# The modulation vector of an adaLN block, computed with its output features on the partitions and moved into two stages of the kernel

## The reference

```python
def adaln_params(cond, w, b):
    mod = jax.nn.silu(cond) @ w + b            # (1024) @ (1024, 6144)
    return jnp.split(mod[..., None, :], 6, axis=-1)

sh1, sc1, g1, sh2, sc2, g2 = adaln_params(c, mod_w[i], mod_b[i])
h_lat = modulate(rmsnorm(x, norm_g[i, 0]), sh1, sc1)      # h * (1 + scale) + shift
x = x + g1 * hyena_mix(h_lat, p)
x = x + g2 * conv_ffn(modulate(rmsnorm(x, norm_g[i, 1]), sh2, sc2), *ffn_p, rows, GRID_W)
```

## Time and profile before

| | |
|---|---|
| median of 3 runs | 1061.96 us (1061.87 to 1062.69) |
| the profiled execution | 1061.37 us |
| its span | 1059.3 us |
| busy share: PE, DVE, ACT, POOL | 98%, 63%, 40%, 51% |
| data moved | 131.9 MB, mean 125 GB/s |

### The profile page before, as it was taken

The page is one execution under the profiler, slowest core; times in us unless marked ns, Lnnn a source line. Parts: engine busy times, 40 slices in busy tenths (PEclk is TensorE's granted clock), DMA queues, the critical chain, the costliest instruction groups (busy, mean ns, idle before and its releaser), DMA issues.

```text
span 1059.3 us, 13471 instructions
## 1 busy us (share of the span) xinstructions
PE 1040.0 (98%) x4968; PEld 856.4 (81%) x4968; DVE 665.7 (63%) x1007; ACT 418.6 (40%) x687; POOL 543.7 (51%) x401
## 2 busy tenths in 40 slices
PE   7999999999999999999999999999999999999996
PEld 5889887877877888778888888778888888888885
DVE  5663776866499765985788847386666666520503
ACT  6223547665554243644444342442323223221222
POOL 1688895999200064234444346535465545553641
PEclk9999999999999999999999999999999999999999
DMA  6446454342446922212322113303222232223222
GB/s 257 164 168 225 133 187 153 90 163 70 179 159 238 379 104 100 93 67 80 110 83 84 54 42 155 143 33 146 87 80 79 103 135 79 80 80 135 104 80 79
DMA packets 19611, 131.92 MB, mean 125 GB/s; under 512 B 3411, under 2 KB 3811, under 8 KB 13030
## 3 DMA queue, kind: packets, MB, share of 16 engines
q1 hardware_dynamic: 8784, 92.62, 23.2%
q0 software_dynamic: 6560, 27.27, 8.0%
q10 hardware_dynamic: 4214, 11.30, 2.8%
HBM read 124.90 MB, written 6.30 MB: 124 GB/s over the span
## 4 chain that ended last, share of the span: by engine, by line
PE 95%; DVE 2%; ACT 1%; DMA 1%; issue 0%; POOL 0%; SPq 0%; POOLq 0%; ACTq 0%; DVEq 0%
PE bank L505 81%; PE bank L496 7%; PE bank L511 3%; PE bank L752 1%; PE bank L746 1%; DMA x_sb<-x_in 1%; PE bank L904 1%; PE bank L741 1%; DVE arena L2178 0%; DVE arena L2181 0%; PE bank L913 0%; PE bank L753 0%; PE bank L869 0%; ACT arena L1189 0%; DVE arena L2214 0%
## 5 line engine op out<-in xcount | busy, mean ns | idle before, releaser
L1730 POOL TENSOR_TENSOR ring_parts<-ring,ring_parts 128x1024 fp32r<-128x1024 f32 x102 | 248.7, 2442 | 266.3 <-ACT ring_parts L1189 263.5
L505 PE MATMUL bank<-hT_parts,ring_parts 128*128 128x512 f32 x1344 | 339.2, 393 | 0.8 <-ACT hT_parts L1518 0.8
L1189 ACT ACTIVATE ring_parts<-ring 128x1024 fp32r<-128x1024 f32 (+2 forms) x163 | 168.6, 1043 | 383.7 <-PE bank L505 219.9
L505 PEld LDWEIGHTS bank<-hT_parts,ring_parts 128*128 128x128 f32 x1344 | 249.6, 188 | 54.7 <-ACT hT_parts L1518 2.4
L505 PE MATMUL bank<-ring_parts,hT_parts 128*128 128x512 f32 (+1 forms) x672 | 171.6, 379 | 1.0 <-POOL ring_parts L1730 0.6
L505 PE MATMUL bank<-ring_parts,arena_parts 128*128 128x512 f32 (+1 forms) x736 | 172.4, 386 | 0.0
L505 PEld LDWEIGHTS bank<-ring_parts,arena_parts 128*128 128x128 f32 x736 | 136.6, 188 | 27.9 <-DVE arena L2416 0.3
L505 PE MATMUL bank<-arena_parts,ring_parts 128*128 128x512 f32 x592 | 148.0, 391 | 0.3 <-DVE arena_parts L2285 0.3
L505 PEld LDWEIGHTS bank<-ring_parts,hT_parts 128*128 128x128 f32 x672 | 122.4, 188 | 22.8 <-POOL ring_parts L1730 1.0
L2521 DVE SCALAR_TENSOR_TENSOR arena<-bank,small,arena 128x441 f32<-128x441 f32 (+2 forms) x176 | 122.3, 695 | 24.6 <-DVE arena L2521 1.7
L505 PEld LDWEIGHTS bank<-arena_parts,ring_parts 128*128 128x128 f32 x592 | 111.0, 188 | 25.4 <-DVE arena_parts L2285 2.1
(11 more groups left out here) (223 smaller groups left out, 1100.5 us busy)
## 6 DMA issues: line engine op xcount, KB each, us to landing
ring<-weights_in SPq DMA_DIRECT2D x39, 2048.0 KB, 8.0
arena<-mod_w_in POOLq DMA_DIRECT2D x32, 512.0 KB, 4.1
arena<-mod_w_in POOLq DMA_DIRECT2D x8, 1024.0 KB, 5.5
x_sb<-x_in SPq DMA_DIRECT2D x4, 512.0 KB, 5.7
ring<-weights_in SPq DMA_DIRECT2D x4, 512.0 KB, 8.5
mod_spill<-mod_part POOLq DMA_DIRECT2D x16, 128.0 KB, 2.1
x_sb<-x_in ACTq DMA_DIRECT2D x4, 512.0 KB, 12.2
arena<-mod_spill ACTq DMA_DIRECT2D x1, 2048.0 KB, 10.6
```

The source lines that it names most:

```text
L505: ins = nc.tensor.matmul(out, l, r, start=start and n == 0, stop=stop and n == len(passes) - 1)
L1189: return nc.scalar.activation(out, in_, ACT.Copy)
L1730: return nc.gpsimd.tensor_tensor(part(low), low, part(high), ALU.subtract)
```

## The change

Weights are laid out so that a tile holds 128 output features on the partitions and the 1024 inputs along the row. One feature's sum is then a sum along the row, and nothing is left to sum over partitions. There are 48 tiles of 128 x 1024 (512 KB). The SiLU of the condition stands as a row on all partitions (`cond_row`).

- GpSimd and ScalarE take 30 tiles: GpSimd multiplies a tile by `cond_row` in place, ScalarE passes over it with a copy that accumulates the sum into one column of `modc` (`mod_sums`). Three buffers: the load of tile j + 2 is issued after the multiply of tile j and waits until tile j - 1 is summed.
- VectorE takes 18 tiles, each with one `scalar_tensor_tensor` that accumulates (`mod_tile`). Two buffers, loaded by GpSimd at fixed places of its loop.
- All of this lies in the gate and merge stages. GpSimd's work in the earlier stages is gone, and so are the spill of the partial sums and its return.
- TensorE's `modulation(j)` and `gate_rows(j)` are gone, as are the copies of their results (`modg_copy`, `modg_late`). The gates go to DRAM as a row of 2048 numbers and return to all partitions by a transfer.

```diff
+MOD_TILES = 6 * KD
+MOD_DVE = 18
+MOD_POOL = MOD_TILES - MOD_DVE
+DVE_LOAD_AFTER = (2, 3, 5, 7, 8, 10, 12, 13, 15, 17, 19, 20, 22, 24, 25, 27)
+MOD_SUMS_AFTER_GATE = (0, 0, 2, 1, 2, 2, 1, 2, 2, 1, 2, 1)
+MOD_SUMS_AFTER_PIECE = (3, 3, 4, 4)
...
+        cond_row = mod_g[:, 0, :]
+        modw_pool = [mod_g[:, 1, :], at(65, D), at(69, D)]
+        modw_dve = [at(75, D), at(79, D)]
...
-            modulation(0)
-            gate_rows(0)
             wo_tile(0)
             wo_tile(1)
-            modulation(1)
-            gate_rows(1)
             filter_tile(0)
             wo_tile(2)
-            modulation(2)
...
             wo_tile(7)
-            gate_rows(2)
-            gate_rows(3)
-            modulation(3)
...
+            def mod_sums(n):
+                for j in range(mod_sums_done[0], mod_sums_done[0] + n):
+                    wait("mod_scaled", j + 1)
+                    w = modw_pool[j % len(modw_pool)]
+                    nc.scalar.activation(w, w, ACT.Copy, accum_out=modc[:, j:j + 1]).then_inc(sem("mod_summed"), 1)
+                mod_sums_done[0] += n
...
                 if u == HEADS:
                     nc.scalar.activation(mgate, mgate, ACT.Silu).then_inc(sem("mgate_ready"), 1)
+                    wait("cond_in", 16)
+                    nc.scalar.activation(cond_row, cond_row, ACT.Silu).then_inc(sem("cond_ready"), 1)
...
                 if i == 2:
                     nc.scalar.activation(sgd[:, 0:4, :], sgd[:, 0:4, :], ACT.Sigmoid).then_inc(sem("sgd_ready"), 1)
+                mod_sums(MOD_SUMS_AFTER_GATE[i])
...
             split_high(FIRST_PD + 4)
-            wait("mod_dve_done", MOD_DVE)
-            act.dma_start(mod_back, mod_spill_d).then_inc(sem("mod_back_in"), 16)
...
+            mod_sums(MOD_SUMS_AFTER_PIECE[0])
+            act.dma_start(minus[:], tables_d[:, 2048:2304]).then_inc(sem("tables_in"), 16)
+            for p in range(FIRST_PD + 5, FIRST_PD + 8):
+                split_high(p)
+                mod_sums(MOD_SUMS_AFTER_PIECE[p - FIRST_PD - 4])
...
+            wait("mod_dve_done", MOD_DVE)
...
+            wait("gates_ready", 1)
+            act.dma_start(mod_row_d.rearrange("a (t p) -> p (a t)", p=P), modc[:, 4 * KD:MOD_TILES],
+                          allow_slow_non_contiguous=True).then_inc(sem("mod_row_out"), 16)
...
             def load_dve(j):
...
+                if j >= len(modw_dve):
+                    wait("mod_dve_done", j - len(modw_dve) + 1)
...
+            wait("cond_ready", 1)
             load_pool(0)
...
+            wait("o_ready", HEADS)
             load_dve(0)
             load_dve(1)
...
+            wait("pv_done", 4 * UNITS)
+            load_pool(1)
+            for j in range(MOD_POOL):
+                b = j % len(modw_pool)
+                wait(f"modw_in{b}", 16 * (j // len(modw_pool) + 1))
+                nc.gpsimd.tensor_tensor(modw_pool[b], modw_pool[b], cond_row, ALU.mult).then_inc(sem("mod_scaled"), 1)
+                if j + 2 < MOD_POOL:
+                    if j:
+                        wait("mod_summed", j)
+                    load_pool(j + 2)
+                if j in DVE_LOAD_AFTER:
+                    load_dve(len(modw_dve) + DVE_LOAD_AFTER.index(j))
...
+            def mod_tile(j):
+                b = j % len(modw_dve)
+                wait(f"modw_dve_in{b}", 16 * (j // len(modw_dve) + 1))
+                c = MOD_POOL + j
+                V.scalar_tensor_tensor(out=modw_dve[b], in0=modw_dve[b], scalar=1.0, in1=cond_row, op0=ALU.mult, op1=ALU.mult,
+                                       accum_out=modc[:, c:c + 1]).then_inc(sem("mod_dve_done"), 1)
...
             for p in range(FIRST_GATE + 6, FIRST_PD + 4):
                 split_low(p)
+                mod_tile(p - FIRST_GATE - 6)
                 if p in (FIRST_GATE + 8, FIRST_GATE + 9):
                     split_output(p - FIRST_GATE + UNITS - 10)
                 if p - FIRST_GATE - 7 in NET_AFTER:
                     net_layer(NET_AFTER.index(p - FIRST_GATE - 7))
-                if p - FIRST_GATE in MOD_AFTER:
-                    mod_chunk(MOD_AFTER.index(p - FIRST_GATE))
...
                 if d % 2:
                     split_low(FIRST_PD + 4 + d // 2)
+                    mod_tile(FIRST_PD - FIRST_GATE - 2 + d // 2)
...
             split_low(FIRST_WO + 3)
...
+            modulation()
```

More of the change, by code:

```diff
@@ L892, in _ @@
                          [(o[0][:, k, :], o[1][:, k, :]) for k in range(HEADS)]).then_inc(sem("merge_done"), 1)
[L895 to L912, removed]
-                nc.tensor.matmul(bank[b], ones_sq, mod_g[:, j // 2, (j % 2) * 512:(j % 2) * 512 + 512],
-                                 start=True, stop=True).then_inc(sem("modg_done"), 1)
             def abs_norm(n):
@@ L1390, in _ @@
             split_high(FIRST_GATE + 7)
-            wait("mod_pool_done", MOD_POOL)
             for i in range(12):
@@ L1767, in _ @@
             load_dve(1)
-            wait("o_turned", UNITS)
-            nc.gpsimd.memset(ones_sq, 1.0).then_inc(sem("ones_ready"), 1)
-            for j in range(2, MOD_DVE):
-                load_dve(j)
+            wait("pv_done", 4 * UNITS)
+            load_pool(1)
+            for j in range(MOD_POOL):
+                b = j % len(modw_pool)
+                wait(f"modw_in{b}", 16 * (j // len(modw_pool) + 1))
[6 more added lines that the diff above has]
+                    load_dve(len(modw_dve) + DVE_LOAD_AFTER.index(j))
@@ L2107, in split_output, with modulation @@
                 V.tensor_tensor(part(low), low, part(high), ALU.subtract).then_inc(sem("oT_low"), 1)
+            def mod_tile(j):
+                b = j % len(modw_dve)
+                wait(f"modw_dve_in{b}", 16 * (j // len(modw_dve) + 1))
+                c = MOD_POOL + j
+                V.scalar_tensor_tensor(out=modw_dve[b], in0=modw_dve[b], scalar=1.0, in1=cond_row, op0=ALU.mult, op1=ALU.mult,
+                                       accum_out=modc[:, c:c + 1]).then_inc(sem("mod_dve_done"), 1)
+            def modulation():
+                wait("mod_summed", MOD_POOL)
+                wait("mod_dve_done", MOD_DVE)
+                V.tensor_tensor(modc[:], modc[:], small[:, SMALL["mod_b"]], ALU.add).then_inc(sem("gates_ready"), 1)
+                wait("gates_ready", 1)
+                for s, name in enumerate(("norm_g1", "norm_g2")):
+                    c = modc[:, (2 * s + 1) * KD:(2 * s + 2) * KD]
+                    ins = V.scalar_tensor_tensor(out=c, in0=c, scalar=1.0, in1=small[:, SMALL[name]], op0=ALU.add, op1=ALU.mult)
+                ins.then_inc(sem("modc_ready"), 1)
             wait("lambda_exps", 1)
@@ L2130, in _ @@
             split_output(UNITS - 3)
-            wait("mod_b_in", 16)
             wait("cond_ready", 1)
```

132 lines of the change are left out of this document (26 added, 106 removed).

## The result

The changed kernel takes 1146.62 us in the median (1145.68 to 1147.98) where the kernel before takes 1062.22 on the same chip: 1.080 times as long, with an interval from 1.078 to 1.081. The prediction was 1136 us with a range from 1100 to 1158, slower with 0.94. The profiled execution took 1146.26 us, its span is 1144.5.

A forecast was written before the change was run, and what follows sets the result against it. PE, busy 98% of the span, was taken as the bound. Stalls of 80.9 us less 2.24, 2.24, 1.70 and 0.7 gave +74.0 on 1061.4, so 1135.4; the median 0.6 above, 1136 us, range 1100 to 1158.

The forecast's parts named there:

- The removed matmuls: The modulation's matmuls on PE's queue, 9.60 us together; taking them off would win about 5 us if all else held.
- Both covers: Removed matmuls hide two waits: 2.24 us ahead of `wo_tile(0)` for copies into `hT`, 3.42 before the second norm's turning.
- The end: Last removed group, 3.42 us, ahead of the second norm's turning; only 0.7 won, because the norm's chain sets the time.
- Steps 1 to 4: Gate stage: queue order delays sums, tiles and first `net_layer`; PE's second network layer stalls 15 us, then `gate_tile(7)` 4.5.
- The gate, merge and `wo_tile(0)` stalls: PE's waits for late pieces and network layers in these stages: 38.8, 30.9 and 11.2 us, 80.9 together.
- The clock: PE's granted clock during stalls: nothing in the sum; upper end allows matmuls a quarter slower through the stretch, +7 us.
- the prediction's marks: Start times carried on once engine, semaphores and load are ready; gate tiles end at 379.3, last merge at 453.7.
- the ring: Gate and merge stages: loop through four queues; POOL multiply 2.40 us, load 4.6, ScalarE sum 1.24, VectorE tile 1.28 to 1.30.
- the turns at the port: VectorE and GpSimd operations with two SBUF operands wait for each other; without this the sum is 17 us less.
- loads land sooner: Rival: no port turns or loads of 4.0 us in these stages; +50 - 2.4, 1109 us; chance 0.17 for 1100 to 1122.
- queues slip less: Rival: only the first stall, 13 to 15 us, and POOL's late tile 29; about 1075 us, chance 0.08.
- the cover is enough: Rival: PE has slack for `net_out` in the gate stage, so the change wins its 5 us: 1057, chance 0.05.

The follow-up runs named there:

- before_no_sums: The kernel before with TensorE's modulation sums cut down to one column or 32 columns, spill, return, copies and waits kept: 1061.26 us, ratio 0.9993.
- after_dve_order: The changed kernel with only VectorE's order changed, each network layer ahead of the tiles at its place and the tiles redistributed: 1120.78 us.
- early_24_later_row: The changed kernel's layout with GpSimd's 24 tiles early and VectorE's 24 in the gate stage, condition row's transfer issued later, third root one block sooner: 1061.98 us.
- after_pool_128: The changed kernel with GpSimd's multiply cut from 1024 columns to 128, all loads, sums, waits and orders kept: 1135.78 us.
- both_orders_pool_128: The changed kernel with VectorE's and ScalarE's orders both mended and GpSimd's multiply cut to 128 of 1024 columns: 1093.17 us.

## Why the prediction was right, step by step

**The removed matmuls.** About 5 us was said; 4.0 to 4.2 were won in the three kernels that have the new sums and no stalls in these stages. Both covers were shown by before_no_sums, the first with another wait than the one described: the prediction read the end of the last copy into `hT` beside the start of `wo_tile(0)` as cause and effect. The end, put at 0.7 of 3.42, gave nothing in before_no_sums, which however keeps VectorE's gate copies.

**The first stall.** Steps 1 to 4 are all in the timelines above, in that order. Tile 0 was summed at 295.1 instead of 293.4, VectorE had its tile 2 at 309.4 instead of 301.6, the second network layer started at 320.55 instead of 315.8. The load was the term that was too small: 4.6 us was assumed, but the one issued at 299.03, 2 us behind a 2 MB chunk, landed after 10.3. VectorE's 18 loads took from 4.2 to 13.3 us, 4.9 in the median. The mechanism is shown by after_dve_order, which changes nothing but the order of VectorE's tiles and network layers.

**The gate, merge and `wo_tile(0)` stalls** were put at 38.8, 30.9 and 11.2 us, 80.9 together. The traced ones are 33.1 (18.24 + 1.81 + 5.22 + 3.24 + 4.59), 19.7 and 7.7: 60.5. **The clock** was put at nothing in the sum and at 7 at most; it cost up to 24.1. Two terms were mis-sized in opposite directions: the stalls 20 us too long, the clock 24 too short. That 60.5 + 24.1 = 84.6 is near 80.9 can have the reason that the prediction gave, a slower matmul filling part of a wait that another engine sets; but no run changes the clock alone, and in early_24_later_row the clock came on top of the wait. So the split was wrong, and that the sum came out within 4 us is in part luck.

**Durations.** The multiply took 2.41 (2.40 said), VectorE's tile 1.23 and 0.08 for reading the sum (1.28 to 1.30), ScalarE's sum 1.04 from start to start (1.24 said; a gap in the rows was taken for cost). VectorE's tiles took 1.94 in the mean, as they met GpSimd's multiplies.

**How much hangs on GpSimd's time.** Here the prediction's marks failed. They gave 28 us for the multiplies' cut where after_pool_128 gave 11, and 23 where both_orders_pool_128 gave 17. They had GpSimd's own time as the longest leg of the ring; in after_pool_128 the waits for loads and for ScalarE's held sums took up most of what the multiplies had given back. For the same reason the 17 us given to the turns at the port are not confirmed as a sum: no run measures them alone, and with nearly all of GpSimd's multiplies gone only 11 us came back in all. That turns are taken is plain in single instructions, 6.92 against 2.77 us. The Trainium skill (SBUF — State Buffer, section "Who interferes with whom") calls the shared pair of ports an exclusive lock; the trace agrees, by those numbers.

**What was not seen at all** is the arena's place, 7.6 us. Without it the kernel stands at 1139.05, 3 us from the forecast, with the luck named above in it. `modc` grew from 32 to 48 columns in plain sight in the diff, and the kernel even has a padding ahead of it to reach a line of 128 bytes; that should have been asked about.

The rivals: "loads land sooner" and "queues slip less" are refuted by the loads and by the later waits; "the cover is enough" by the 18.24 us.

## What to carry over

Work that is moved into a stage where the bounding engine has no slack has to be followed through every queue it enters. What cost most here was neither the length of the new operations nor their number, but one small operation (a network layer, a sum) queued behind a tile whose load waited, through two more queues, for that same operation. Reordering alone gave back 36 of 84 us. And when a kernel gets slower in stages that the change does not touch, compare the mean duration of one group of instructions there, and look at what moved in memory.

## What the runs showed of the hardware that was not expected

- fp32r matmuls of 128 x 512 with an operand in a buffer that begins at 115392 or 115456 bytes took 392 ns in the mean of 736, at 115328 or 115584 386 ns; the whole kernel differed by 7.6 and 7.8 us. A 128-byte line was not enough, a shift by 256 changed nothing.
- The granted clock was 0.74 to 0.94 in the stretches between 320 and 480 us, though PE's single waits there were 1 to 5 us long. Slower matmuls made up to 24 us of the changed kernel's time beside the waits. In early_24_later_row one wait of 3.97 us left the marks 6.3 us late.
- The 512 KB load that was issued at 429.16, just behind a 2 MB chunk and a 1 MB load, took 13.3 us to land, where the median of VectorE's 18 is 4.9.
- Three VectorE subtractions that met a GpSimd multiply and four additions took 6.92 us instead of 2.77, and the additions 4.79 instead of the 3.06 of the block before.
